# RMS-norm sums on TensorE: 32-column ones as the stationary side, or the squares themselves with one column of ones moving

## What is computed

```
def rms_norm(x, g, eps):
    y = xf * lax.rsqrt(jnp.mean(xf * xf, axis=-1, keepdims=True) + eps)
    return (y * g).astype(x.dtype)

def first_block(x, ...):
    for l in range(DEPTH):                        # DEPTH = 2
        h = rms_norm(x, norm_mix_pre[l], NORM_EPS)
        m = hybrid_mixer(h, ...)
        x = x + rms_norm(m, norm_mix_post[l], NORM_EPS)
        h = rms_norm(x, norm_ffn_pre[l], NORM_EPS)
        f = swiglu(h, w_gate_up[l], w_down[l])
        x = x + rms_norm(f, norm_ffn_post[l], NORM_EPS)

def second_block(x, ...):
    for l in range(DEPTH):
        h = rmsnorm(x, g_mix[l]) * (1.0 + sc1) + sh1
        ...                                       # four mixers; mla norms cq (256 wide) and ckv (128 wide)
        x = x + gt1 * (mix @ w_out[l])
        h = rmsnorm(x, g_ffn[l]) * (1.0 + sc2) + sh2
        f = (silu(h @ ffn_w1[l]) * (h @ ffn_w3[l])) @ ffn_w2[l]
        x = x + gt2 * f
    return rmsnorm(x, g_final)
```

## Time and profile before

| | |
|---|---|
| median of 3 runs | 3305.64 us |
| lowest, highest | 3304.11, 3306.10 us |
| profiled execution, own time | 3304.82 us |
| its span, first to last instruction | 3303.0 us |
| TensorE matmul busy | 3211.5 us, 97% |
| VectorE, ScalarE, GpSimd busy | 49%, 41%, 42% |
| mean granted TensorE clock | 0.993 of full |

### The profile page before, as it was taken

The page is one execution under the profiler, slowest core; times in us unless marked ns, Lnnn a source line. Parts: engine busy times, 40 slices in busy tenths (PEclk is TensorE's granted clock), DMA queues, the critical chain, the costliest instruction groups (busy, mean ns, idle before and its releaser), DMA issues. The chain is left out here.

```text
span 3303.0 us, 45719 instructions
## 1 busy us (share of the span) xinstructions
PE 3211.5 (97%) x16045; PEld 2562.3 (78%) x16045; DVE 1631.5 (49%) x2602; ACT 1341.9 (41%) x2106; POOL 1378.2 (42%) x696
## 2 busy tenths in 40 slices
PE   8999999999998999999999999999999999999998
PEld 6778887788886678887788886767888867778887
DVE  6843337656626833337655624863333249533332
ACT  6755554322226755554322224554222244532222
POOL 3233333544443233333544444534444435444444
PEclk9999999999999999999999999999999999999999
DMA  3122222255532122222255533202233332123333
GB/s 132 57 80 86 86 79 70 89 200 182 204 106 73 57 80 86 79 86 69 91 187 194 203 103 104 78 26 77 95 96 102 102 110 71 39 77 96 100 101 103
DMA packets 94307, 335.31 MB, mean 102 GB/s; under 512 B 11072, under 2 KB 12288, under 8 KB 93952
## 3 DMA queue, kind: packets, MB, share of 16 engines
q1 hardware_dynamic: 92480, 327.65, 30.0%
q10 hardware_dynamic: 1728, 6.36, 0.5%
HBM read 331.83 MB, written 8.44 MB: 103 GB/s over the span
## 5 line engine op out<-in xcount | busy, mean ns | idle before, releaser
L436 POOL TENSOR_TENSOR wLo<-wring,wHi 128x1024 fp32r<-128x1024 f32 x482 | 1174.3, 2436 | 1743.9 <-ACT wHi L416 1743.7
L460 PE MATMUL psG<-hHi,wHi 128*128 128x512 f32 x2992 | 1185.9, 396 | 9.6 <-DVE ra L1284 2.7
L460 PE MATMUL psG<-hLo,wHi 128*128 128x512 f32 x2992 | 1171.6, 392 | 8.8 <-POOL hLo L485 7.9
L460 PE MATMUL psG<-hHi,wLo 128*128 128x512 f32 x2992 | 1167.2, 390 | 0.0
L416 ACT ACTIVATE wHi<-wring 128x1024 fp32r<-128x1024 f32 x482 | 510.2, 1059 | 982.9 <-PE psG L460 936.0
L460 PEld LDWEIGHTS psG<-hHi,wHi 128*128 128x128 f32 x2992 | 563.1, 188 | 148.2 <-issue 22.9
L460 PEld LDWEIGHTS psG<-hLo,wHi 128*128 128x128 f32 x2992 | 562.4, 188 | 139.9 <-POOL hLo L485 21.9
L460 PEld LDWEIGHTS psG<-hHi,wLo 128*128 128x128 f32 x2992 | 563.5, 188 | 113.5 <-issue 0.5
L460 PE MATMUL psG<-hidLo,wHi 128*128 128x512 f32 x704 | 274.1, 389 | 0.0
L460 PE MATMUL psG<-hidHi,wHi 128*128 128x512 f32 x704 | 274.1, 389 | 0.0
L460 PE MATMUL psG<-hidHi,wLo 128*128 128x512 f32 x704 | 274.1, 389 | 0.0
(11 more groups left out here) (321 smaller groups left out, 3428.8 us busy)
## 6 DMA issues: line engine op xcount, KB each, us to landing
wring<-in_w SPq DMA_DIRECT2D x494, 512.0 KB, 3.6
modw<-in_wmod SPq DMA_DIRECT2D x96, 512.0 KB, 5.3
e_copies<-e_rows ACTq DMA_DIRECT2D x8, 512.0 KB
T_tab<-e_copies SPq DMA_DIRECT2D x4, 1024.0 KB, 5.6
mask<-in_mask SPq DMA_DIRECT2D x2, 1536.0 KB, 6.0
xin_sb<-in_x SPq DMA_DIRECT2D x4, 512.0 KB, 5.0
e_copies<-e_rows ACTq DMA_DIRECT2D x8, 256.0 KB
out<-o_sb SPq DMA_DIRECT2D x4, 512.0 KB, 3.7
```

The lines of the kernel that those rows point to most:

```text
L436: pool.tensor_tensor(wLo[:, c % CUTS, :, :], wring[:, c % RING, :, :], wHi[:, c % CUTS, :, :], ALU.subtract).then_inc(w_cut[c % CUTS], 1)
L460: mm = pe.matmul(psG[:, G.slot(u), :], w[:, c % CUTS, k, :], r(j), start=start and j == 0 and n == 0, stop=stop and j == len(kts) - 1 and ...
```

## The change

- The sums (`token_sums`, in place of `quarter_sums`) take 128 tokens' squares, 128 by 128, as the stationary side and one column of ones as the moving side. The sum of token a·128+p lands on partition p, column a of `psT`; there are still 4 products (8 passes) for a tile.
- Root and inverse are taken on 128 by 4 instead of 128 by 128, at all norms, the latent ones too (there ScalarE's copy as well).
- The spread has column a of the inverse, broadcast to 128 by 128, as the stationary side and the identity as the moving side. The matrix `spread` and its memsets are gone.
- In `norm_pe_sum` the sum of `acc` is issued as soon as the last tile has been taken out of PSUM, and only the sum of the last square waits for `acc_full`.
- In the last block of code the inverse is already a column: the transpose and the copy to `r_col` go, and row 3 is transposed together with the others instead of behind them.

```diff
-        def quarter_sums(pe, tt, parts, start=True, stop=True):
+        def token_sums(pe, tt, parts, start=True, stop=True):
+            for j, s in enumerate(parts):
+                for a in range(TT):
+                    mm = pe.matmul(psT[:, T.slot(tt), a:a + 1], s[:, a * P:(a + 1) * P], ones[:, 0:1],
+                                   start=start and j == 0 and a == 0, stop=stop and j == len(parts) - 1 and a == TT - 1)
+            return mm
+
+        def spread(pe, tt, r):
             for a in range(TT):
-                for j, s in enumerate(parts):
-                    mm = pe.matmul(psT[32 * a:32 * a + 32, T.slot(tt), 0:P], ones[:, 0:32], s[:, a * P:(a + 1) * P],
-                                   start=start and j == 0, stop=stop and j == len(parts) - 1)
+                mm = pe.matmul(psT[:, T.slot(tt), a * P:(a + 1) * P], r[:, a:a + 1].to_broadcast([P, P]), ident[:, :], start=True, stop=True)
             return mm
...
-        def norm_pe_sum(pe, tt, n):
-
+        def norm_pe_sum(pe, tt, n, u):
+
+            pe.wait_ge(*G.is_read(u))
+            pe.wait_ge(*T.is_free(tt))
+            token_sums(pe, tt, (acc,), stop=False)
             pe.wait_ge(acc_full, KT * n)
-            pe.wait_ge(*T.is_free(tt))
-            quarter_sums(pe, tt, (acc, squares[1])).then_inc(T.filled(tt), 1)
+            token_sums(pe, tt, (squares[1],), start=False).then_inc(T.filled(tt), 1)
...
-            act.activation(root(tt), psT[:, T.slot(tt), 0:P], ACT.Sqrt, bias=eps[:, 0:1], scale=1.0 / width).then_inc(rms_full, 1)
+            act.activation(root(tt), psT[:, T.slot(tt), 0:TT], ACT.Sqrt, bias=eps[:, 0:1], scale=1.0 / width).then_inc(rms_full, 1)
...
             def _(pe):
-                pe.transpose(psT[:, 1, 0:P], inv(0), ident[:, :]).then_inc(rstd_full, 1)
                 for k in range(KT):
                     pe.wait_ge((h_high, h_full)[k % 2], k // 2 + 1)
-                    for a in range(TT - 1):
+                    for a in range(TT):
                         mm = pe.transpose(rows[a][:, k * P:(k + 1) * P], x_out[:, k, a * P:(a + 1) * P], ident[:, :])
                         if k == KT - 1:
                             mm.then_inc(o_full, 1)
-                pe.wait_ge(rs_full, 1)
-                for k in range(KT):
-                    mm = pe.transpose(rows[TT - 1][:, k * P:(k + 1) * P], x_out[:, k, (TT - 1) * P:TT * P], ident[:, :])
-                mm.then_inc(o_full, 1)
```

More of the change, by code:

```diff
@@ L341, in root @@
         def root(tt):
-            return rstd[:, 2 * P * T.slot(tt):2 * P * T.slot(tt) + P]
+            return rstd[:, 2 * P * T.slot(tt):2 * P * T.slot(tt) + TT]
         def inv(tt):
-            return rstd[:, 2 * P * T.slot(tt) + P:2 * P * T.slot(tt) + 2 * P]
-        spread = sb("spread", [P, TT, P])
+            return rstd[:, 2 * P * T.slot(tt) + P:2 * P * T.slot(tt) + P + TT]
         acc, squares = sq[:, 0, :], (rms[:, :], sq[:, 1, :])
@@ L558, in norm_pe_spread @@
             pe.wait_ge(inv_full, r + 1)
-            for a in range(TT):
-                mm = pe.matmul(psT[:, T.slot(tt), a * P:(a + 1) * P], spread[:, a, :], inv(tt), start=True, stop=True)
-            mm.then_inc(rstd_full, 1)
+            spread(pe, tt, inv(tt)).then_inc(rstd_full, 1)
         def norm_act_quarters(act, tt, width=DM):
             act.wait_ge(*T.is_full(tt))
-            act.activation(root(tt), psT[:, T.slot(tt), 0:P], ACT.Sqrt, bias=eps[:, 0:1], scale=1.0 / width).then_inc(rms_full, 1)
+            act.activation(root(tt), psT[:, T.slot(tt), 0:TT], ACT.Sqrt, bias=eps[:, 0:1], scale=1.0 / width).then_inc(rms_full, 1)
         def norm_dve_inverse(dve, tt, n):
@@ L678, in _ @@
                 dve.memset(tick[:, :], 0.0)
-                did(dve.memset(spread[:, :, :], 0.0))
-                for a in range(TT):
-                    did(dve.memset(spread[32 * a:32 * a + 1, a, :], 1.0))
                 for k in range(KT):
@@ L699, in _ @@
                 act.wait_ge(pro_sum, KT)
-                act.activation(root(0), psT[:, 0, 0:P], ACT.Sqrt, bias=eps[:, 0:1], scale=1.0 / DM).then_inc(pro_root, 1)
+                act.activation(root(0), psT[:, 0, 0:TT], ACT.Sqrt, bias=eps[:, 0:1], scale=1.0 / DM).then_inc(pro_root, 1)
             @block.gpsimd
@@ L956, in _ @@
                     keep_awake(pe, 6)
[L957 removed]
+                    norm_pe_sum(pe, t_N2, 1, g_WO + KT - 1)
                     keep_awake(pe, 5)
@@ L1516, in program @@
         rec, var, rs = sb("rec", [P, 2, HEADS], blk), sb("var", [P, 16], blk), sb("rs", [P, 16], blk)
-        half, r_col = sb("half", [P, 1], blk), sb("r_col", [P, TT], blk)
+        half = sb("half", [P, 1], blk)
         vT = sq
@@ L1754, in _ @@
                                 pe.wait_ge(*T.is_free(tr[name]))
[L1755 to L1758, removed]
+                                spread(pe, tr[name], c_inv[:, j, 0:TT]).then_inc(T.filled(tr[name]), 1)
                             second_half(TILE_AT[s])
@@ L1811, in _ @@
                     keep_awake(pe, 11)
-                    norm_pe_sum(pe, t_X, 1)
+                    norm_pe_sum(pe, t_X, 1, g_DN2 + KT - 1)
                 @block.scalar
@@ L2312, in _ @@
                 scaled_tile(7)
-                dve.wait_ge(rstd_full, 1)
-                dve.tensor_copy(r_col[:, :], psT[:, 1, 0:P].rearrange("p (a b) -> p a b", a=TT)[:, :, 0]).then_inc(rs_full, 1)
-                dve.wait_ge(rs_full, 1)
                 for a in (1, 3):
                     dve.wait_ge(o_full, a + 1)
-                    dve.tensor_scalar(o_sb[:, a, :], rows[a], r_col[:, a:a + 1], None, ALU.mult).then_inc(o_rest, 1)
+                    dve.tensor_scalar(o_sb[:, a, :], rows[a], inv(0)[:, a:a + 1], None, ALU.mult).then_inc(o_rest, 1)
             @block.sync
```

17 lines of the change are left out of this document (8 added, 9 removed).

## The result

The changed kernel takes 3353.95 us (median of four runs, 3352.52 to 3360.07) against 3305.07 us before: a ratio of 1.0151, interval 1.0134 to 1.0169. The page, whose second row gives busy time, share of the span and instructions of each engine, answers to the earlier trace rows: TensorE's busy time has grown by 63 us (3211.5 to 3274.4), the span by 55.

The account below looks back on a forecast made before the run. TensorE, busy 97% of the span, was taken to bound the kernel. Places summed to +14.2 us at unchanged clock, +44.4 with clock falls; 3304.8 + 44.4 = 3349.2 profiled, the median 0.8 above, so 3350 us, range 3314 to 3360.

Parts of the forecast that it names:

- a fall of the clock: Likeliest case: TensorE's clock falls in tile sums and prologue, +44.4 us in all, 3350 us; chance 0.55.
- latent sums: Two latent layers: TensorE some 1.75 us more, VectorE freed of 1.5; between -1.5 and +1.8 a layer, taken as 0.
- last block: Row 0 complete with the 29th transpose, not the 22nd, delaying ScalarE's first copy: 0.3 to 1.5 us, taken as +1.2.
- price of a pass: Every norm sum: a 128-column load sets 0.112 us a pass, so a tile's sum holds TensorE 0.90 us against 0.35.
- Root and inverse: All 13 chains: inverse 0.77 us shorter, root 0.16, together 0.93 each; 12.1 us if all stood on the path.
- Post sums: Four post sums: the spread stands behind the keep-awakes, 616.7 against 616.69, so nothing is won: 0.
- Tile sums at full clock: Four tile sums with the clock as before: +1.8 us each with spread (two), +1.5 each before a barrier (two).
- The clock: Tile sums and prologue: with almost nothing moving the clock falls, first three sums at full clock, five at half.
- prologue: Prologue sums: +2.0 us with the clock as before, +7.4 with the clock's fall.
- places before a barrier: Two tile sums ahead of a barrier: +1.5 us each with the clock as before, +6.7 each with its fall.
- tile sums with spread: Two tile sums followed by a spread: +1.8 us each with the clock as before, +9.0 each with its fall.
- clock holds: Rival for the whole kernel: loading weights keeps the clock up, +14.2 us, 3320 us (3314 to 3325); chance 0.30.

Follow-up runs that it names:

- e1_wide: The changed kernel with all 128 columns of ones moving in each pass of a norm sum instead of one: 3319.77 us, ratio 1.0048.
- e2_wide_few: e1_wide with the keep-awakes ahead of the eight spreads cut from 5 products to 1: 3316.46 us, ratio 1.0035.
- e5_before_few: The kernel before the change with only the eight keep-awake blocks ahead of the spreads cut from 5 products to 1: 3306.30 us, ratio 1.0001.
- e3_tile_old: The changed kernel with the tile sums with spread, their root, inverse and spread made as before: 3335.48 us, ratio 1.0093.
- e7_wide_latent_old: e1_wide with the latent layers' two small norms made as before: 3316.86 us, ratio 1.0037.
- e8_awake4: The changed kernel with 4 keep-awakes instead of 1 between sums in the four tile sums, none between the last two: 3359.83 us, ratio 1.0164.
- e9_awake5_all: The changed kernel with 5 keep-awakes between all sums of the four tile sums, the last two included: 3368.99 us, ratio 1.0177.
- e6_single: e1_wide with squares and ones as float32r, one pass a product instead of two, keep-awakes left at 5: 3300.54 us, ratio 0.9981.

## Why the prediction was right, and where not

The forecast was 3350 us by a fall of the clock, 3314 to 3360; it came to 3353.95, and the mechanism is the forecast one. That it came within 4 us owes something to luck: the latent sums cost 4 us or more that stood at nothing, and against them stand the last block, 1.1 us under its forecast, and falls of the clock from before that did not recur (2.3 us in the trace), which no term held. By its own steps:

- **The price of a pass**, 0.112 us taken from loads with 65 moving columns: measured 0.112 with one. Full width costs the same, as e1_wide shows. By the issue floor that the Trainium skill states (TensorE: Matmul & The Clock Gate, Back-to-back issue gap), about 25 ns for a product of so few columns, an estimate of eight passes would be 0.2 us; the trace has 0.97. The same section says that this gap has no load of weights in it, and that in a stream of loads and products both set the spacing; here the load does. The Trainium skill (the same page, LDWEIGHTS) gives a load as its columns over 1.2 GHz, 0.107 us for 128; at full clock the trace is near it, with 0.112. At a granted clock of 0.50 it is not: a sum and a keep-awake, ten passes, start 2.14 us apart, 0.214 us a pass.
- **Root and inverse**: the inverse gained 0.77 us, as forecast (953 to 178 ns). The root gained 0.10 and not 0.16: it went from 367 to 264 ns, and I had taken for it the 204 ns of another function, an exponential of 128 by 2 (line 995 of the kernel before). The Trainium skill (ScalarE: Activation LUTs, What ACT_TABLE_LOAD costs) gives an activation with its bias in a column of memory as 280 ns and 0.833 ns for each element, and says that such a column adds 93 ns to one without; the estimates by it are 283 and 387 ns, and the trace is near, with 264 and 367. By the code the exponential is given no bias column, and the root is. Over thirteen places that is 0.8 us of gain that was never there.
- **Post sums, keep-awakes eat the gain**: right, +0.1 a place instead of 0, and e2_wide_few and e5_before_few show both halves of it.
- **Tile sums at full clock**: +1.8 and +1.5 forecast, +1.8 and +1.5 to +1.6 in e1_wide.
- **The clock**: it fell in all five places named. I gave three sums at full clock; the tile sums had one and a half to four and the prologue one. That makes the prologue +8.5 instead of +7.4, and the two places before a barrier +5.1 and +7.8 instead of 6.7. At the tile sums with spread it is +9.0 and +9.6 for 9.0, of which 0.97 and 0.96 come behind the start of the spread, for 0.9 forecast. What the kernel loses there goes with the place (e3_tile_old).
- **Latent sums**: wrong. I had the bounds -1.5 and +1.8 and took the middle, "both are busy there". e7_wide_latent_old shows 2.0 us a layer, above the upper bound: TensorE ends last there and VectorE's time counts for nothing. The fall of the clock there (+6 in the first layer of the profiled execution) was not foreseen. With the same sums there, e3_tile_old has none and e8_awake4 has one in the other layer, so it comes and goes.
- **Last block**: mis-sized, +0.1 for +1.2. The clock was at 1.00 for the first eight transposes and fell at 3346.2; the bound 0.3 for a clock that is up was nearer.
- **The rival "clock holds"** had the right arithmetic, +14.2, for a kernel that was not this one: e1_wide is that kernel, at +14.0, with the latent term (+4.0) made good by the last block and by falls of before that did not recur. Its reason, that loading weights keeps the clock, was wrong: the clock fell and stayed down while PEld was never idle. How much movement it takes is not known from these runs, since full products between the one-column sums did not reliably keep it up (e8_awake4, e9_awake5_all).

## What to carry to other kernels

Count what a matrix product loads and what it moves, apart. Turning an operand to the stationary side puts 128 new weight columns in each pass, which here had the price of a full pass however few columns moved, and with one column moving the clock fell; so before such a turn ask which engine ends last at each place, and move full-width columns where the passes are paid anyway. When a later step is shortened, look at what is queued ahead of its consumer on the same engine: here keep-awakes swallowed the gain until they were cut with it.

## What the runs showed of the hardware

- A pass with 128 weight columns costs 0.112 us at full clock with 1, 65 or 128 columns moving, as float32 (two passes a product: 8 in 0.97 us) and as float32r (one pass: 4 in 0.52 us).
- Weight loads back to back did not hold TensorE's clock here: it was at 0.50 through 7.40 us with PEld busy in 7.40, and stayed there through 25.00 us of one-column sums and keep-awakes by turns. The same mixture kept 1.00 through 14.85 us at another place of the same execution. With full-width sums it was 1.00 in every tile sum, but in the prologue it fell to 0.50 in two of four traces of the float32r kernels (8.20 us of e6_single).
- A pass with 128 weight columns takes 0.214 us at a granted clock of 0.50 (ten in 2.14 us), so the load follows the clock.
- A square root of 128 by 4 on ScalarE takes 264 ns and one of 128 by 128 367 ns: 32 times fewer elements save 0.10 us. A reciprocal on VectorE goes from 953 to 178 ns.
